# Three transformer blocks on one core: the norms' per-token sums kept as columns, the next norm's sum derived from known sums, and the first unit after a norm from raw fp32 weights

## The chip, the cores and the metric

The kernel runs on one core of a Trainium2 chip, in one launch. Its time is the device time in microseconds, the median of several executions. The engines of the core work in parallel and wait for each other through semaphores: TensorE (PE) multiplies, VectorE (DVE) and ScalarE (ACT) work element by element, GpSimd (POOL) does too, and SyncE (SP) issues the transfers from memory. TensorE's results go to PSUM, which has eight banks of 128x512 fp32 here; everything else lies in SBUF.

## The reference

One sequence of 512 tokens, 1024 channels, all in fp32. A first block (a modulated norm, a mixer of dilated attention and a state-space branch, a modulated norm, a feed-forward block with a short convolution) ends with a norm of its own. Then follow two layers of the second kind:

```
def _rmsnorm_2(x, g):
    y = x32 * lax.rsqrt(jnp.mean(x32 * x32, axis=-1, keepdims=True) + RMS_EPS)
    return (y * g.astype(jnp.float32)).astype(x.dtype)

def second_block(...):
    for l in range(DEPTH_2):
        g = norm_g[l]
        f = _swiglu(_rmsnorm_2(x, g[0]), ffn_w_gate[l, 0], ffn_w_up[l, 0], ffn_w_down[l, 0])
        x = x + 0.5 * _rmsnorm_2(f, g[1])
        m = _mixer(_rmsnorm_2(x, g[2]), w_in[l], conv_w[l], pool_w[l], pool_scale[l], w_out[l])
        x = x + _rmsnorm_2(m, g[3])
        f = _swiglu(_rmsnorm_2(x, g[4]), ffn_w_gate[l, 1], ffn_w_up[l, 1], ffn_w_down[l, 1])
        x = x + 0.5 * _rmsnorm_2(f, g[5])
    return x
```

The norms are per token, over the channels. Between the output of one part and the input of the next stand two of them: the one of `f` (or `m`), which needs all of `f`, and the one of the new `x`, which needs the update by the first. The seven places where this happens are called norms 0 to 6 here: norm 0 is the first block's final norm together with the first norm of layer 0; norms 1, 2, 3 stand behind the first feed-forward block, the mixer and the second feed-forward block of layer 0; norms 4, 5, 6 behind those of layer 1. Norm 6 is the end of the kernel and has no next norm.

## The kernel before

**Layout.** Channels lie on the 128 partitions and the 512 tokens along the free axis, so `x`, `f` and `u` are 8 chunks of 128x512. A sum over channels therefore runs across partitions and chunks.

**Split products.** Every large product is done in a rounded fp32 form (fp32r) with both factors split into a high and a low part: for each chunk of 128 input channels three matmuls of 128x128 by 128x512, `w_hi*u_hi`, `w_hi*u_lo` and `w_lo*u_hi` (L381 to L383). A *unit* is all of these for one 128-channel output, summed in one bank, `unit_bank[0]` or `[1]`. Two units are a *pair*, one for each of two weight slots. A unit over 8 chunks has 24 matmuls. Some small sums are done in plain fp32, where a matmul shows as two instructions.

**Weights.** SyncE loads each unit's weights to `raw[s]`. ScalarE rounds them to `w_hi` (`refill`, L699), once TensorE has finished with the slot. GpSimd subtracts, `w_lo = raw - w_hi` (`split_pair`, L332). The unit on TensorE waits for that and for its bank to have been taken by VectorE (`taken`).

**A feed-forward block of the two layers** runs in two halves of 11 hidden chunks. The hidden units come as pairs (gate, up); VectorE multiplies both by `rstd`, the per-token factor of the norm (L1415, L1417), ScalarE applies the activation and rounds (`h_hi`, L905), and VectorE subtracts for `h_lo` (L1422). The factor is applied to the outputs of the units because the units read x times the gain, without it. Then `down` runs 8 units over the 11 chunks of the half. VectorE takes each bank: `f` is copied in the first half (L1396), added in the second (L1393). **The mixer** has 10 input pairs, attention, convolution and pooling between them, and an output projection of 8 units over 8 chunks, whose banks are copied to `f` (L1396). The first block has a feed-forward block of the same shape with 8 chunks a half.

**A norm** (1 to 5). While the last 8 units run, ScalarE squares each taken chunk (L880) and VectorE adds the square to `acc` (L1400). After the last, TensorE sums `acc` over the partitions with a matrix of ones (`f_sum`, L441), so that each of 128 rows of `stat_bank` has all 512 sums. ScalarE takes the root (L709), VectorE the reciprocal of 128x512 (L1116) and then, for each chunk, the update: `f*g*rstd` to a buffer (L1376) and its addition to `x` (L1377). Behind each updated chunk ScalarE rounds `x*gain` to `u_hi` (L869) and squares `x` (L705), VectorE subtracts for `u_lo` (L1362, `low_part`), and GpSimd adds the squares (`add_squares`, L344 and L347). TensorE runs the first pair chunk by chunk, as the chunks come, into the banks `score`, holding both weight slots until its end (`first_pair`, L420 to L422); behind it the sum of squares of `x` (L427), from which ScalarE and VectorE make the next `rstd`. Norm 0 differs: the products of `down` are written over `x` (L1306), and the squares of `x` are summed by TensorE in fp32 between the units (`unit_and_square`); final norm at L1351. Norms 3 and 0 end in the head of a loop turn over the layers.

**What sets the order.** It is written out by hand: one program per engine, in which a semaphore count stands before each step. SyncE's queue is in the order of use and waits for a `raw` slot. Loops over layers, halves and units are hardware loops.

## Time and profile before

| | |
|---|---|
| runs | 2871.98, 2873.22, 2876.57 us |
| median | 2873.22 us |
| span of the profiled execution | 2864.1 us |
| TensorE busy, matmul | 2611.8 us, 91% |
| TensorE weight loads, beside the matmuls | 2053.4 us, 72% |
| VectorE busy | 1366.7 us, 48% |
| ScalarE busy | 915.4 us, 32% |
| GpSimd busy | 1071.6 us, 37% |

The page gives no time for the profiled execution other than its span, which leaves out what lies around the program. In a timeline every line is one instruction or a row of equal ones: its start in us from the start of the span, its length, the engine, the line in the code, output and inputs, the shape and the count. In brackets stands the idle time of the engine just before, with the operation that ended it. PEclk is the granted clock of TensorE as a share of full speed.

### The profile page before, as it was taken

How to read it: one execution, taken by the hardware profiler on the slowest of the kernel's cores; microseconds unless marked ns; L12 is line 12 of the kernel's file. 1: busy time of each engine (PE TensorE's matmuls, PEld its weight loads, DVE VectorE, ACT ScalarE, POOL GpSimd, SP SyncE). 2: the span in 40 equal slices, each digit the busy share in tenths (PEclk: the TensorE clock that was granted, in tenths of full speed). 3: DMA queues.
4: the chain of work that ended last, by engine and by line, in shares of the span. 5: the costliest groups of instructions: out<-in, count | busy, mean ns of one | idle time of the engine just before them, and what ended most of it. 6: DMA issues, size and time to landing. Idle time of an engine off the chain costs nothing.

```text
span 2864.1 us, 34463 instructions
## 1 busy us (share of the span) xinstructions
PE 2611.8 (91%) x11068; PEld 2053.4 (72%) x11068; DVE 1366.7 (48%) x1956; ACT 915.4 (32%) x1265; POOL 1071.6 (37%) x436
## 2 busy tenths in 40 slices
PE   4988888999799999799799999599997999799997
PEld 2566676888678887576578888488885676588885
DVE  6887667535342232766443132532234656532233
ACT  3333333523332232443332232322233442332231
POOL 1222233444444444322344444344444222444442
PEclk8899899999899999999899999799999999999998
DMA  4111145222123222111122222122231111123231
GB/s 199 52 51 51 42 173 196 95 95 95 59 95 107 84 102 89 45 51 52 66 81 102 89 98 100 46 95 103 89 107 61 52 59 52 66 95 103 88 106 70
DMA packets 63564, 247.74 MB, mean 86 GB/s; under 512 B 7056, under 2 KB 7056, under 8 KB 62224
## 3 DMA queue, kind: packets, MB, share of 16 engines
q1 hardware_dynamic: 63504, 247.01, 24.7%
q8 instruction: 29, 0.48, 0.1%
q14 instruction: 31, 0.25, 0.0%
HBM read 244.89 MB, written 2.10 MB: 86 GB/s over the span
## 4 chain that ended last, share of the span: by engine, by line
PE 66%; issue 21%; DVE 6%; POOL 5%; ACT 1%; DVEq 0%; POOLq 0%; ACTq 0%
PE unit_bank L381 21%; PE unit_bank L383 21%; PE unit_bank L382 21%; POOL w_lo L332 3%; POOL arena L347 2%; PE out_bank L488 1%; DVE rstd L1116 1%; PE score L478 1%; DVE arena L1033 1%; PE score L475 1%; DVE arena L1507 1%; DVE arena L1505 1%; DVE arena L1494 0%; DVE arena L1495 0%; DVE arena L1376 0%
## 5 line engine op out<-in xcount | busy, mean ns | idle before, releaser
L332 POOL TENSOR_TENSOR w_lo<-raw,w_hi 128x1024 fp32r<-128x1024 f32 (+2 forms) x390 | 1006.0, 2581 | 1695.6 <-ACT w_hi L699 1695.6
L381 PE MATMUL unit_bank<-u_hi,w_hi 128*128 128x512 f32 x2160 | 858.5, 397 | 27.5 <-POOL w_lo L332 18.7
L382 PE MATMUL unit_bank<-u_lo,w_hi 128*128 128x512 f32 x2160 | 849.0, 393 | 0.0
L383 PE MATMUL unit_bank<-u_hi,w_lo 128*128 128x512 f32 x2160 | 848.3, 393 | 0.0
L699 ACT ACTIVATE w_hi<-raw 128x1024 fp32r<-128x1024 f32 (+2 forms) x390 | 430.0, 1105 | 1129.9 <-PE unit_bank L383 1083.3
L381 PEld LDWEIGHTS unit_bank<-u_hi,w_hi 128*128 128x128 f32 x2160 | 410.7, 190 | 140.5 <-POOL w_lo L332 27.9
L383 PEld LDWEIGHTS unit_bank<-u_hi,w_lo 128*128 128x128 f32 x2160 | 410.3, 190 | 87.2
L382 PEld LDWEIGHTS unit_bank<-u_lo,w_hi 128*128 128x128 f32 x2160 | 410.7, 190 | 85.6 <-issue 1.4
L381 PE MATMUL unit_bank<-h_hi,w_hi 128*128 128x512 f32 x992 | 390.6, 394 | 5.3 <-DVE h_lo L1566 3.6
L382 PE MATMUL unit_bank<-h_lo,w_hi 128*128 128x512 f32 x992 | 386.7, 390 | 0.0
L383 PE MATMUL unit_bank<-h_hi,w_lo 128*128 128x512 f32 x992 | 386.6, 390 | 0.0
L1417 DVE TENSOR_TENSOR arena<-unit_bank,rstd 128x512 f32<-128x512 f32 x84 | 58.1, 692 | 397.7 <-PE unit_bank L383 397.7
L381 PEld LDWEIGHTS unit_bank<-h_hi,w_hi 128*128 128x128 f32 x992 | 186.5, 188 | 48.4 <-DVE h_lo L1566 4.4
L382 PEld LDWEIGHTS unit_bank<-h_lo,w_hi 128*128 128x128 f32 x992 | 186.7, 188 | 40.0 <-issue 1.7
L383 PEld LDWEIGHTS unit_bank<-h_hi,w_lo 128*128 128x128 f32 x992 | 186.6, 188 | 39.1
L1422 DVE TENSOR_TENSOR h_lo<-arena,h_hi 128x512 f32 (+1 forms) x88 | 169.9, 1931 | 79.2 <-ACT h_hi L905 79.2
L1396 DVE COPY f<-unit_bank 128x512 f32 x48 | 33.2, 692 | 250.0 <-PE unit_bank L383 250.0
L420 PE MATMUL score<-u_hi,w_hi 128*128 128x512 f32 x96 | 46.0, 479 | 100.7 <-DVE u_lo L1362 100.5
L1415 DVE TENSOR_TENSOR arena<-unit_bank,rstd 128x512 f32<-128x512 f32 x84 | 58.1, 691 | 112.3 <-PE unit_bank L383 112.3
L880 ACT ACTIVATE arena<-f 128x512 f32 (+1 forms) x48 | 30.3, 632 | 251.0 <-DVE f L1393 184.3
L420 PEld LDWEIGHTS score<-u_hi,w_hi 128*128 128x128 f32 x96 | 20.7, 215 | 122.7 <-DVE u_lo L1362 119.3
L1393 DVE TENSOR_TENSOR f<-unit_bank,f 128x512 f32 x32 | 22.2, 693 | 152.4 <-PE unit_bank L383 152.4
(238 smaller groups left out, 2370.5 us busy)
## 6 DMA issues: line engine op xcount, KB each, us to landing
raw<-in_w_gate_up SPq DMA_DIRECT2D x176, 512.0 KB, 3.2
raw<-in_w_down SPq DMA_DIRECT2D x64, 704.0 KB, 4.0
raw<-in_w_in SPq DMA_DIRECT2D x70, 512.0 KB, 3.2
f<-in_w_ada_rows SPq DMA_DIRECT2D x32, 512.0 KB, 4.9
raw<-in_w_up SPq DMA_DIRECT2D x32, 512.0 KB, 3.3
raw<-in_w_out SPq DMA_DIRECT2D x24, 512.0 KB, 3.3
ada_w<-in_w_ada SPq DMA_DIRECT2D x8, 1024.0 KB, 7.4
raw<-in_w_down SPq DMA_DIRECT2D x16, 512.0 KB, 3.3
```

Of the source, the lines that this page charges most:

```text
L332: e.tensor_tensor(w_lo[:, s, 0:n], raw[:, s, 0:n], as32(w_hi[:, s, 0:n]), ALU.subtract).then_inc(lo_ready, 1)
L347: e.tensor_tensor(acc, acc, sq[:, c % 2, :], ALU.add).then_inc(sq_used, 1)
L381: e.matmul(bank[:], wh, hi(k), start=n == 0, stop=False)
L382: e.matmul(bank[:], wh, lo(k), start=False, stop=False)
L383: mm = e.matmul(bank[:], wl, hi(k), start=False, stop=last)
L420: e.matmul(into[s][:], wh, u_hi[:, c, :], start=c == 0, stop=False)
L699: e.activation(w_hi[:, s, 0:n], raw[:, s, 0:n], ACT.Copy).then_inc(hi_ready, 1)
L880: e.activation(sq[:, 0, :], f[:, bass.ds(c, 1), :].rearrange("p a t -> p (a t)"), ACT.Square).then_inc(fsq_ready, 1)
L1396: e.tensor_copy(fc, unit_bank[s][:]).then_inc(taken[s], 1)
L1415: e.tensor_tensor(ffn_g, banks[0][:], rstd[:], ALU.mult).then_inc(taken[0], 1)
L1417: e.tensor_tensor(ffn_u, banks[1][:], rstd[:], ALU.mult).then_inc(taken[1], 1)
L1422: e.tensor_tensor(flat(h_lo[:, bass.ds(i, 1), :]), ffn_h, as32(flat(h_hi[:, bass.ds(i, 1), :])), ALU.subtract).then_inc(h_ready, 1)
```

## The change

**Sums as columns.** `sq`'s place in the buffers is divided anew. Each norm's sums are now done with the data as the stationary operand and one column of ones as the moving one (`token_sums`): four products, one for each 128 tokens, give a [128, 4] tile with one token per partition. The root and the reciprocal work on this tile. Where the factor is needed along the free axis, `spread` multiplies the broadcast column by the identity, four products of 128 columns, which gives the 128x512 form in PSUM.

**The next norm's sum from known sums.** With new `x` = `x + g*f*inv`, the sum of squares of the new `x` is the old sum plus 2 times the sum of `x*g*f` times `inv` plus the sum of `(g*f)^2` times `inv` squared. So while the last 8 units run, ScalarE makes a second square, `(g*f)^2` (`gf_sq`), and VectorE adds it to `gf_acc`, makes `x*g*f` (`cross`) and adds that to `cross_acc`; for norm 0 only `gf` is there. `add_squares` and the squares of `x` are gone, and the old sum is kept in `x_sum`. The last chunk's square of `f` is summed by its own products and not added to `f_acc` first.

**The first unit pair in fp32.** The raw weights of the first pair of each part go by transfers of their own (`load_first`) to `first_raw`, a stage ahead, and stay unsplit. `u_all` holds x times the gain in fp32. The pair is 16 plain fp32 products into the `score` banks. The two weight slots pass it by, so the pairs behind it are counted one fewer per part. `u_hi` is rounded from `u_all` by ScalarE, and the eight subtractions for `u_lo` stand behind all eight updates. The first half of the update is written to a `unit_bank` in PSUM instead of a buffer in SBUF, and reads the factor from `stat_bank`.

The loops over the layers are written out, and the activation tables are loaded at set places.

```diff
+        f_sq, gf_sq, f_acc, cross, cross_acc, gf_acc = (slot(n) for n in range(6))
+        f_sum, root_f, root_u, inv_f, inv_u, grown = (slot(11)[:, 128 + 4 * n:132 + 4 * n] for n in range(6))
+        x_sum = stat[:, 0:TB]
+        u_all = slots(16, 8)
+        first_raw = arena[:, 12 * T:16 * T].rearrange("p (s n) -> p s n", s=2)
...
+            def load_first(m, w, first):
+                for s in range(2):
+                    if m:
+                        e.wait_ge(first_done, 2 * (m - 1) + s + 1)
+                    e.dma_start(first_raw[:, s, :], w[first + s]).then_inc(first_loaded[s], 16)
...
+                        e.wait_ge(cat_ready, 4 * l + 4)
+                        load_first(3 * l + 2, d["w_gate_up"], 4 * HALF2 * (2 * l + 1))
+                        load_pairs(mix2(l) + MIX2_IN + 2, d["w_out2"], DC * l + 4, DC // 2 - 2)
...
-                            split_pair(ffn2(l, s), D)
-                            add_squares(3 + 3 * l + 2 * s)
...
+            def token_sums(bank, at, src, apart=1):
+                for b in range(TB):
+                    n = at + apart * b
+                    mm = e.matmul(bank[:, n:n + 1], src[:, b * P:(b + 1) * P], tab("ones", 0, 1), start=True,
+                                  stop=True)
+                return mm
+            def spread(n, inv, bank):
+                e.wait_ge(inverse_ready, n)
+                for b in range(TB):
+                    mm = e.matmul(bank[:, b * P:(b + 1) * P], inv[:, b:b + 1].broadcast_to([P, P]), tab("ident"),
+                                  start=True, stop=True)
+                mm.then_inc(spread_ready, 1)
+            def norm(r):
+                e.wait_ge(fsq_added, (DC - 1) * (r + 1))
+                token_sums(out_bank, 0, f_acc, 2)
+                e.wait_ge(fsq_ready, 2 * DC * r + (2 if r < NORMS - 1 else 1) * (DC - 1) + 1)
+                token_sums(out_bank, 1, f_sq, 2).then_inc(sums_ready, 1)
+                spread(2 * r + 1, inv_f, stat_bank)
+                if r == NORMS - 1:
+                    return
+                e.wait_ge(cross_ready, r + 1)
+                mm = token_sums(mix[0], 0, gf_acc)
+                if r:
+                    mm = token_sums(mix[0], TB, cross_acc)
+                mm.then_inc(cross_sums, 1)
+                for s in range(2):
+                    e.wait_ge(first_loaded[s], 16 * (r + 1))
+                for c in EIGHT:
+                    e.wait_ge(u_full, DC * r + c + 1)
+                    for s in range(2):
+                        mm = e.matmul(score[s][:], first_raw[:, s, c * P:(c + 1) * P], u_all[:, c, :],
+                                      start=c == 0, stop=c == DC - 1)
+                        if c == DC - 1:
+                            mm.then_inc(first_done, 1)
+                    if c == 5:
+                        spread(2 * r + 2, inv_u, mix[1])
...
-                            first_pair(p0, 2 + 3 * l + k_norm, 3 + 3 * l + k_norm, score)
-                            in_unit(p0 + 1, 0, free=0)
-                            in_unit(p0 + 1, 1, free=0)
+                            unit(p0 + 1, 0, from_u, from_u_lo, EIGHT, before=u_chunk(3 * l + k_norm))
+                            in_unit(p0 + 1, 1)
...
-                    f_sum(3 * l + k_norm)
+                    norm(3 * l + k_norm + 1)
...
+            def token_root(out, src):
+                e.activation(out, src, ACT.Sqrt, bias=eps[:], scale=1.0 / D).then_inc(root_ready, 1)
+            def f_squares(p, s, part, c, g):
+                e.wait_ge(taken[s], p + 2)
+                settled()
+                fc = part[:, bass.ds(c, 1), :].rearrange("p a t -> p (a t)")
+                e.activation(f_sq, fc, ACT.Square).then_inc(fsq_ready, 1)
+                if g is not None:
+                    e.activation(gf_sq, fc, ACT.Square, scale=g(c)).then_inc(fsq_ready, 1)
+            def norm(r, p, part, g):
+                ahead = r < NORMS - 1
+                g = g if ahead else None
+                with e.Fori(0, DC // 2 - 1) as i:
+                    for s in range(2):
+                        f_squares(p + i, s, part, 2 * i + s, g)
+                        refill(p + i + 1, s, D if r in (2, 5) or r == 0 else RING)
+                p = p + DC // 2 - 1
+                f_squares(p, 0, part, DC - 2, g)
+                if ahead:
+                    refill(p + 1, 0)
+                f_squares(p, 1, part, DC - 1, g)
+                e.wait_ge(f_summed, r + 1)
+                token_root(root_f, f_sum)
+                if not ahead:
+                    return
+                refill(p + 1, 1)
+                for c in range(DC):
+                    e.wait_ge(x_ready, DC * r + c + 1)
+                    e.activation(u_all[:, c, :], x[:, c, :], ACT.Identity,
+                                 scale=col("norm_g", 2 * r * DC + c)).then_inc(u_full, 1)
+                    e.wait_ge(u_full, DC * r + c + 1)
+                    e.activation(u_hi[:, c, :], u_all[:, c, :], ACT.Copy).then_inc(uhi_ready, 1)
+                    if c == 3:
+                        e.wait_ge(grown_ready, r + 1)
+                        token_root(root_u, grown)
+                e.wait_ge(spread_ready, 2 * r + 2)
+                e.activation(rstd[:], mix[1][:], ACT.Copy).then_inc(rstd_ready, 1)
...
+            def norm(r, p, take, part, g, update):
+                ahead, crossed = r < NORMS - 1, 0 < r < NORMS - 1
+                e.memset(f_acc, 0.0)
+                if ahead:
+                    e.memset(gf_acc, 0.0)
+                if crossed:
+                    e.memset(cross_acc, 0.0)
...
+                def add_gf(c):
+                    e.wait_ge(fsq_ready, 2 * (DC * r + c) + 2)
+                    step(e.tensor_tensor(gf_acc, gf_acc, gf_sq, ALU.add))
+                def chunk(p, s, c, last):
+                    e.wait_ge(unit_done, 2 * p + s + 1)
+                    take(p, s, c)
+                    if crossed:
+                        e.wait_ge(taken[s], p + 2)
+                        settled()
+                        step(e.scalar_tensor_tensor(cross, row(x, c), g(c), row(f, c), ALU.mult, ALU.mult))
+                        step(e.tensor_tensor(cross_acc, cross_acc, cross, ALU.add))
+                    if last:
+                        return
+                    e.wait_ge(fsq_ready, 2 * DC * r + (2 if ahead else 1) * c + 1)
+                    step(e.tensor_tensor(f_acc, f_acc, f_sq, ALU.add))
+                    if ahead:
+                        add_gf(c)
+                    e.sem_inc(fsq_added, 1)
+                with e.Fori(0, DC // 2 - 1) as i:
+                    turn = step.enter(i, 2 * ((2 if crossed else 0) + 1 + ahead))
+                    for s in range(2):
+                        chunk(p + i, s, 2 * i + s, False)
...
+                p = p + DC // 2 - 1
+                chunk(p, 0, DC - 2, False)
+                chunk(p, 1, DC - 1, True)
+                e.wait_ge(sums_ready, r + 1)
+                e.tensor_reduce(f_sum, out_bank[:, 0:2 * TB].rearrange("p (b n) -> p b n", n=2),
+                                mybir.AxisListType.X, ALU.add).then_inc(f_summed, 1)
+                e.wait_ge(root_ready, 2 * r + 1)
+                e.reciprocal(inv_f, root_f).then_inc(inverse_ready, 1)
+                if ahead:
+                    add_gf(DC - 1)
+                    e.sem_inc(cross_ready, 1)
+                e.wait_ge(spread_ready, 2 * r + 1)
+                for c in range(DC):
+                    update(c)
+                    if c == 1 and ahead:
+                        e.wait_ge(cross_sums, r + 1)
+                        gf_sum, cross_sum = mix[0][:, 0:TB], mix[0][:, TB:2 * TB]
+                        step(e.tensor_tensor(grown, gf_sum, inv_f, ALU.mult))
+                        if r:
+                            step(e.scalar_tensor_tensor(grown, cross_sum, 2.0, grown, ALU.mult, ALU.add))
+                            step(e.tensor_tensor(grown, grown, inv_f, ALU.mult))
+                            step(e.tensor_tensor(x_sum, x_sum, grown, ALU.add))
+                        else:
+                            step(e.tensor_tensor(x_sum, grown, inv_f, ALU.mult))
+                        e.tensor_copy(grown, x_sum).then_inc(grown_ready, 1)
+                    if c == 5 and ahead:
+                        e.wait_ge(root_ready, 2 * r + 2)
+                        e.reciprocal(inv_u, root_u).then_inc(inverse_ready, 1)
+                if not ahead:
+                    return
+                for c in range(DC):
+                    e.wait_ge(uhi_ready, DC * (2 + r) + c + 1)
+                    e.tensor_tensor(u_lo[:, c, :], u_all[:, c, :], as32(u_hi[:, c, :]),
+                                    ALU.subtract).then_inc(u_ready, 1)
+                e.wait_ge(rstd_ready, r + 1)
...
+            def post_norm(g):
+                def update(c):
+                    step(e.scalar_tensor_tensor(unit_bank[c % 2][:], f[:, c, :], g(c), stat_bank[:], ALU.mult,
+                                                ALU.mult))
+                    e.tensor_tensor(x[:, c, :], unit_bank[c % 2][:], x[:, c, :], ALU.add).then_inc(x_ready, 1)
+                return update
```

In the instructions of TensorE, the end of the first feed-forward block of layer 0 (norm 1) reads so before; `arena` is the buffer that holds `acc`, and `tabs` the ones:

```order
L383 MATMUL unit_bank<-h_hi,w_lo 128x512
L434 REGISTER_ALU
L434 COMPARE_AND_BRANCH
L440 ISA
L441 MATMUL stat_bank<-arena,tabs 128x512
L413 ISA
L415 REGISTER_ALU
L417 REGISTER_ALU
L420 MATMUL score<-u_hi,w_hi 128x512
L421 MATMUL score<-u_lo,w_hi 128x512
L422 MATMUL score<-u_hi,w_lo 128x512
```

and so after, where `out_bank` receives the sums of `f` and `mix` those for the next norm, then the second factor, and `score<-arena` is the fp32 pair:

```order
L402 MATMUL unit_bank<-h_hi,w_lo 128x512
L498 REGISTER_ALU
L498 COMPARE_AND_BRANCH
L449 MATMUL out_bank<-tabs,arena 128x1 x8
L457 MATMUL stat_bank<-tabs,arena 128x128 x4
L449 MATMUL mix<-tabs,arena 128x1 x8
L483 MATMUL score<-arena 128x512 x12
L457 MATMUL mix<-tabs,arena 128x128 x4
L483 MATMUL score<-arena 128x512 x4
L400 MATMUL unit_bank<-u_hi,w_hi 128x512
L401 MATMUL unit_bank<-u_lo,w_hi 128x512
L402 MATMUL unit_bank<-u_hi,w_lo 128x512
```

The single wide sum is replaced by 8 one-column products and a spread, 8 more one-column products stand before the first pair, the pair has 16 products and a second spread inside it, and the first ordinary unit follows it directly, with no sum between.

VectorE, one chunk of the mixer's output projection (norm 2) before:

```order
L1396 ISA
L1396 COPY f<-unit_bank 128x512
L1398 ISA
L1399 ISA
L1400 TENSOR_TENSOR arena<-arena 128x512
L1391 REGISTER_ALU
```

and after, where the second row is the take, `x,cols,f` makes `cross`, and the adds are those of `cross_acc`, `f_acc` and `gf_acc`:

```order
L1504 ISA
L1504 COPY f<-unit_bank 128x512
L1438 REGISTER_ALU
L1440 ISA
L1440 SCALAR_TENSOR_TENSOR arena<-x,cols,f 128x512
L91 ISA
L1441 TENSOR_TENSOR arena<-arena 128x512
L91 REGISTER_ALU
L1444 ISA
L1445 TENSOR_TENSOR arena<-arena 128x512
L91 REGISTER_ALU
L1431 ISA
L1432 TENSOR_TENSOR arena<-arena 128x512
```

Between one take and the next VectorE has four further steps where it had one.

VectorE between the last take of norm 1 and its first updates, before:

```order
L1388 REGISTER_ALU
L1388 COMPARE_AND_BRANCH
L1115 REGISTER_ALU
L1116 RECIPROCAL rstd<-arena 128x512
L90 REGISTER_ALU
L1376 ISA
L1376 SCALAR_TENSOR_TENSOR arena<-f,half_g,rstd 128x512
L90 REGISTER_ALU
L1377 TENSOR_TENSOR x<-x,arena 128x512
```

and after:

```order
L1500 TENSOR_TENSOR f<-unit_bank,f 128x512
L1440 SCALAR_TENSOR_TENSOR arena<-x,half_g,f 128x512
L1441 TENSOR_TENSOR arena<-arena 128x512
L1459 TENSOR_REDUCE arena<-out_bank 128x4
L1462 RECIPROCAL arena<-arena 128x4
L1432 TENSOR_TENSOR arena<-arena 128x512
L1517 SCALAR_TENSOR_TENSOR unit_bank<-f,half_g,stat_bank 128x512
L1519 TENSOR_TENSOR x<-unit_bank,x 128x512
```

The wide reciprocal gives way to a reduction and a reciprocal of 128x4; two cross steps stand ahead of them, the last add of `gf_acc` behind them, and the update's first half goes to PSUM.

## Rows read from the trace of the kernel before

**Rows 1.** Busy time by stretches: length, then PE, PEld, DVE, ACT, POOL, PEclk, DMA, GB/s

```profile
core 0 of [0], span 2864.1 us
800.00:1138.00 338.00, 338.00 (x1493) 279.88 (x1492) 100.40 (x106) 91.92 (x104) 149.90 (x56) 1.00 0.28 97
...
1138.00:1193.00 55.00, 35.57 (x129) 23.55 (x128) 42.57 (x61) 23.93 (x40) 20.36 (x11) 0.88 0.13 47
```

**Rows 2.** Timeline of TensorE at norm 1: start, us, operation, [idle before <- what ended it]

```profile
1138.55 0.39 PE L383 MATMUL unit_bank<-h_hi,w_lo 128*128 128x512 f32 x1
1141.32 2.07 PE L441 MATMUL stat_bank<-arena,tabs 128*128 128x512 f32 x2 [2.38 <-DVE arena L1400]
1151.25 0.79 PE L420 MATMUL score<-u_hi,w_hi 128*128 128x512 f32 x1 [7.85 <-DVE u_lo L1362]
...
1154.86 0.39 PE L421 MATMUL score<-u_lo,w_hi 128*128 128x512 f32 x1
...
1175.66 0.50 PE L381 MATMUL unit_bank<-u_hi,w_hi 128*128 128x512 f32 x1 [2.12 <-POOL w_lo L332]
```

**Rows 3.** Timeline of VectorE and ScalarE at the same norm, columns as before

```profile
1139.10 0.69 DVE L1393 TENSOR_TENSOR f<-unit_bank,f 128x512 f32 x1 [5.24 <-PE unit_bank L383]
...
1139.83 0.63 ACT L880 ACTIVATE arena<-f 128x512 f32<-128x512 f32 x1 [5.89 <-DVE f L1393]
...
1144.15 3.35 DVE L1116 RECIPROCAL rstd<-arena 128x512 f32<-128x512 f32 x1 [2.88 <-ACT arena L709]
1147.67 0.75 DVE L1376 SCALAR_TENSOR_TENSOR arena<-f,half_g,rstd 128x512 f32<-128x512 f32 x1 [0.16 <-DVE rstd L1116]
1148.45 0.69 DVE L1377 TENSOR_TENSOR x<-x,arena 128x512 f32<-128x512 f32 x1
...
1149.32 0.72 ACT L869 ACTIVATE u_hi<-x,cols 128x512 fp32r<-128x512 f32 x1 [4.25 <-DVE x L1377]
```

**Rows 4.** Timeline of VectorE and TensorE at norms 0, 3 and 5

```profile
756.68 0.75 DVE L1306 SCALAR_TENSOR_TENSOR x<-unit_bank,mod,x 128x512 f32 x1 [5.60 <-PE unit_bank L383]
...
790.43 0.50 PE L381 MATMUL unit_bank<-u_hi,w_hi 128*128 128x512 f32 x1 [2.12 <-POOL w_lo L332]
...
1794.55 0.69 DVE L1393 TENSOR_TENSOR f<-unit_bank,f 128x512 f32 x1 [5.24 <-PE unit_bank L383]
...
1842.41 0.50 PE L381 MATMUL unit_bank<-u_hi,w_hi 128*128 128x512 f32 x1 [2.12 <-POOL w_lo L332]
...
2457.74 0.69 DVE L1396 COPY f<-unit_bank 128x512 f32 x1 [3.19 <-PE unit_bank L383]
...
2493.37 0.50 PE L381 MATMUL unit_bank<-u_hi,w_hi 128*128 128x512 f32 x1 [2.12 <-POOL w_lo L332]
```

**Rows 5.** Timeline: short fp32 sums on TensorE and one small VectorE add

```profile
41.72 6.99 PE L531 MATMUL out_bank<-tabs,ada_acc 128*128 128x1 f32 x32 [14.81 <-DVE ada_acc L1097]
48.74 0.17 DVE L1103 TENSOR_TENSOR mod<-out_bank,cols 128x16 f32<-128x16 f32 x1 [7.08 <-PE out_bank L531]
...
491.23 1.84 PE L539 MATMUL out_bank<-tabs,ada_sums 128*128 128x1 f32 x16
...
787.29 1.02 PE L427 MATMUL stat_bank<-arena,tabs 128*128 128x512 f32 x2
...
1358.61 1.88 PE L512 MATMUL score<-arena,pool_w 128*128 128x512 f32 x4
```

**Rows 6.** Timeline of ScalarE and GpSimd in the mixer's output projection

```profile
1381.51 0.63 ACT L880 ACTIVATE arena<-f 128x512 f32 x1 [3.85 <-DVE f L1396]
1382.05 1.04 ACT L699 ACTIVATE w_hi<-raw 128x1024 fp32r<-128x1024 f32 x1
...
1383.17 2.40 POOL L332 TENSOR_TENSOR w_lo<-raw,w_hi 128x1024 fp32r<-128x1024 f32 x1 [3.04 <-ACT w_hi L699]
```

**Rows 7.** Timeline of GpSimd and VectorE in a hidden stage

```profile
1458.28 2.54 POOL L332 TENSOR_TENSOR w_lo<-raw,w_hi 128x1024 fp32r<-128x1024 f32 x1 [2.97 <-ACT w_hi L699]
...
1459.48 1.88 DVE L1422 TENSOR_TENSOR h_lo<-arena,h_hi 128x512 f32 x1 [0.92 <-ACT h_hi L905]
```

302 lines of the change are left out of this document (129 added, 173 removed).

## The prediction

> **What bounds the kernel now.** I read the span and the busy time by stretches first, then the timeline of one norm. In the hidden and down products of a feed-forward block TensorE is busy for the whole stretch, 338.0 of 338 us. The 55 us at a norm hold 35.6 us of busy TensorE at a granted clock of 0.88 [rows 1]. So time can be won only at the seven norms, and any delay put into the stretches between them is paid in full.
>
> The timeline of the norm at 1139 us shows what a norm costs. The last product of the down projection starts at 1138.55 and takes 0.39 us, so I count from E = 1138.94. TensorE then runs one sum, starts the first pair at 1151.25 and the first ordinary unit at 1175.66 [rows 2], which is 36.7 us after E. Only 48 products of 0.227 us, 10.9 us, lie in it. The rest is a chain [rows 3]: take of the last bank (0.16 us after E), square, add, the fp32 sum on TensorE, square root, a reciprocal over 128x512 of 3.35 us, the first update at E + 8.7, and the first rounded chunk at E + 10.4. Then the first pair goes at VectorE's pace, and after it the two weight slots that it held are split again: the last idle before 1175.66 is 2.12 us for `w_lo` [rows 2].
>
> The other norms read the same way. The take starts 0.16 us after E, so E follows from it. Of the four norms of this pattern (r = 1, 2, 4, 5) the first needs 36.7 us and the last, 2457.58 to 2493.37, 35.8 us; the mean of the four is 36.2. Norm 3, between the layers, needs 1794.39 to 1842.41, 48.0 us. Norm 0 needs 756.52 to 790.43, 33.9 us [rows 4].
>
> **The change, part by part.** I build the new stretch from E to the first ordinary unit.
>
> 1. Start of the chain. The take and the square are as before: the square ends at E + 1.52 [rows 3]. The sums of the seven earlier chunks run meanwhile. The last square is summed by four one-column products, 8 instructions: 0.115 us each warm, 0.22 us each cold [rows 5], 0.9 or 1.8 us. The clock is at half in the old sum at 1141.32, since its two instructions take 2.07 us against 1.02 warm [rows 2, 5], so it falls about there: I take the middle, E + 2.9.
> 2. The reduction, the root and the reciprocal work on 128x4 in place of 128x512. No such row exists; the nearest is an add of 128x16 from PSUM, 0.17 us [rows 5]. With hand-overs of 0.05 us the three take 0.75 us: E + 3.65. The 3.35 us reciprocal is gone.
> 3. The spread of the inverse is 8 instructions of 128 columns, bounded by 0.115 each (one column, warm) and a quarter of a cold 512-column one (1.03 / 4 = 0.26). I take 0.25, cold: E + 5.65. Norm 6 ends with its updates from here; they stood at E + 8.7, so the tail shortens by 3.0 us.
> 4. Before the first pair TensorE also sums `gf_acc` and `cross_acc`, 16 one-column instructions, 3.5 us cold: E + 9.2. In norm 0 only 8 of them stand there: E + 7.4. The first update and add (0.75 + 0.69) and ScalarE's 0.72 give the first chunk of u by E + 8 [rows 3], so the sums decide.
> 5. The first pair is now 16 fp32 products, 32 instructions. Two take 1.02 us and four 1.88 [rows 5], so one more costs 0.43, and 32 of them 13.8 us in place of 10.9. The clock: before, the first pair starts cold at 1151.25 and is warm (0.39 us) at 1154.86, at most 3.6 us later [rows 2]. Where the rise falls hangs on chance, so I take somewhat more, 4.2 us (bounds 3 and 6); at half speed 2.1 us of them are lost. The second spread adds 0.95. Sum 16.8 us: E + 26.0, in norm 0 E + 24.2.
> 6. VectorE is not later. An update and its add are 1.44 us, the step between them 0.03 [rows 3]; eight from E + 5.65, with 1.5 us of small steps, end at E + 19. The eight subtractions for `u_lo` (0.69 each) then run ahead of TensorE, which needs the first at E + 26. GpSimd no longer adds up the squares of x, and so doesn't collide with VectorE there. The weights of the next pair are split early, since the first pair no longer holds their slots; the 2.12 us wait goes. If VectorE had to write the updates to PSUM at more than 2.2 us each, it would be the bound (a rival).
>
> Gains: four norms at 36.2 - 26.0 = 10.2, 40.8 us; norm 3 at 48.0 - 26.0 = 22.0; norm 0 at 33.9 - 24.2 = 9.7; the tail 3.0. In the down products of norm 0, TensorE also loses the interleaved fp32 sums: chunks come every 5.60 + 0.75 = 6.35 us (the wait for the bank and its take) [rows 4], against 24 x 0.2264 = 5.43 for 24 products by [rows 1], where 1493 take 338 us. Five such periods are 4.6 us. Together 80.1 us.
>
> 7. What the down products pay. Each chunk now has a second square on ScalarE ahead of the weights' rounding, and up to three more VectorE steps. In the output projection of the mixer, 8 k-tiles, a unit is 5.43 us. Rounding starts 0.54 us after the square and `w_lo` 1.12 us after that, for 2.40 us [rows 6]. With the square at 0.73 after the take the split ends 4.8 us after it; a second square makes that 5.4, and the weights are needed 5.3 after it. Norm 0 has the same: about 0.2 us for six units, 1.2 us. The 11 k-tiles of the feed-forward blocks (7.47 us a unit) have room.
> 8. In the mixer's output VectorE itself is the larger cost. After the take come cross (0.75), its add, the f add and the gf add, each 0.69 with about 0.15 between in the loop: the gf add would start 3.4 us after the take, just after `w_lo` starts (3.2). An `h_lo` subtraction of two SBUF inputs that starts inside a `w_lo` of 1458.28 to 1460.82 takes 1.88 us instead of 0.69 and ends 0.54 us after it [rows 7]. So I let the gf add end 0.5 us after a split that ends at 5.7: the next take comes 6.2 us after this one, where 5.43 were due. Over seven chunks this is 5.1 us, in each of two mixers. In the feed-forward blocks the same add ends at 7.4 us, within the 7.47. Losses: 10.2 + 1.2 = 11.4 us.
>
> The row shows the add held until the split ends. The Trainium skill, page "SBUF — State Buffer", section "Who interferes with whom", says the same as a rule: the shared port pair belongs to whichever of the two starts first, for its whole instruction. By it point 8 costs 5.1 us a mixer; if both engines simply ran side by side it would cost only the 1.2 us of point 7, and the sum would be 7.8 us lower. It also speaks against this change in one more place, the last gf add at a norm: should the split of slot 1 start before it, all that follows moves by 1.9 us.
>
> Other edits cost nothing: the first weights are two loads more to a queue with DMA engines idle for most of the time, issued a stage ahead (in the mixer after `cat_ready`, eight units or 43 us before use); the table loads are moved under the down products; the loop over layers is written out, one more fetch of instructions; memsets (0.48 each) fall into VectorE's wait before the first chunk.
>
> **The sum.** 2864.1 - 80.1 + 11.4 = 2795.4 us of span. The page gives no time for the profiled execution beyond its span; the median of the runs, 2873.22, is 9.1 above it. I predict 2804.5 us.
>
> **The rivals.**
> - *The clock stays up.* If the small sums are enough to keep it, or it returns earlier, points 1, 3, 4 and 5 lose 0.3, 1.1, 1.7 and 2.1 us: 5.2 a norm, 31 us over six, 2773. Against it: one-column products ran for 7 us at 0.22 us each without becoming faster [rows 5].
> - *VectorE becomes the bound.* Updates that write to PSUM have no row. At 0.69 + 0.75 they are hidden; at 2.4 us an update pair, or with the last gf add locked out, a norm costs 2 to 4 us more: 2817 to 2829.
> - *The fp32 pair stays cold* (slower than before). If the clock didn't return during it, its 32 instructions cost 27.6 us in place of 15.9, the second spread 1 us more, and the next unit starts cold, 2 us more: 14.6 a norm, 88 us over six, 2892. It decides from a first pair of over 27 us. Against: the earlier first pair warmed within 3.6 us, though VectorE made it wait in between.
> - *The change is hidden by the weights.* If something else released the first ordinary unit (its weights, or the `u_lo` of the last chunks) the norms would stay near 36 us, and only the tail and norm 0 would win: 2873.2 - 7.6 + 11.4 = 2877. Nothing in the rows points there.
>
> **How the numbers follow.** Chances: the forecast (2790 to 2817) 0.62, the clock up 0.15, VectorE bound 0.15, cold 0.05, hidden 0.03. The range from 2776 to 2832 takes in the first three nearly whole. About 0.2% is what a measurement of this kernel can tell from no change: faster by more 0.92, within it 0.03, slower 0.05.
>
> **What would show it.** From the last product of a down projection to the first ordinary unit 26 us (24 in norm 0); the first fp32 product at about E + 9, the last warm; chunks of the mixer's output every 6.2 us; the gf add of those chunks at about 2.8 us instead of 0.69; the first update at E + 5.7. Wrong: a first pair that waits for `u_all` (VectorE bound), a wait for `w_lo` in the feed-forward down products, or a start of the chain at full clock.

## The result: 2799.22 us, 2.6% less, and the profile after

The changed kernel takes 2799.22 us (median of 4 runs, 2793.74 to 2800.65) where the kernel before took 2874.89 in the same series: ratio 0.9739, 95% interval 0.9718 to 0.9759. The forecast was 2804.5, with a range of 2776 to 2832. The profiled execution has a span of 2796.1 us, 68.0 less than before; the sum in the prediction gave 2795.4.

The busy time of two stretches of the changed kernel, the columns as in [rows 1], which they answer:

```profile
core 0 of [0], span 2796.1 us
790.00:1128.00 338.00, 338.00 (x1490) 279.11 (x1489) 115.56 (x128) 98.27 (x114) 152.44 (x56) 1.00 0.30 99
1132.00:1187.00 55.00, 53.47 (x212) 36.42 (x211) 42.10 (x97) 28.15 (x54) 7.11 (x3) 0.94 0.12 39
```

Between the norms of the feed-forward blocks nothing has changed: TensorE is busy throughout, at full clock (a granted clock of 1.00, that is 2.4 GHz; *warm* below means this, *cold* means half of it). The 55 us from norm 1 on hold 53.5 us of TensorE instead of 35.6. TensorE at that norm, which answers [rows 2]:

```profile
1133.12 0.95 PE L449 MATMUL out_bank<-tabs,arena 128*128 128x1 f32 x8
1134.73 1.05 PE L449 MATMUL out_bank<-tabs,arena 128*128 128x1 f32 x8 [0.66 <-ACT arena L768]
1136.65 1.47 PE L457 MATMUL stat_bank<-tabs,arena 128*128 128x128 f32 x8 [0.87 <-DVE arena L1462]
1137.91 3.41 PE L449 MATMUL mix<-tabs,arena 128*128 128x1 f32 x16
1141.18 12.03 PE L483 MATMUL score<-arena 128*128 128x512 f32 x24
1153.05 1.05 PE L457 MATMUL mix<-tabs,arena 128*128 128x128 f32 x8
1153.93 3.60 PE L483 MATMUL score<-arena 128*128 128x512 f32 x8
1156.97 0.79 PE L400 MATMUL unit_bank<-u_hi,w_hi 128*128 128x512 f32 x1
```

and VectorE there, which answers [rows 3]:

```profile
1133.32 0.69 DVE L1500 TENSOR_TENSOR f<-unit_bank,f 128x512 f32<-128x512 f32 x1 [3.82 <-PE unit_bank L402]
...
1135.89 0.17 DVE L1459 TENSOR_REDUCE arena<-out_bank 128x4 f32<-128x8 f32 x1 [0.36 <-PE out_bank L449]
1136.42 0.18 DVE L1462 RECIPROCAL arena<-arena 128x4 f32<-128x4 f32 x1 [0.36 <-ACT arena L761]
...
1138.15 0.76 DVE L1517 SCALAR_TENSOR_TENSOR unit_bank<-f,half_g,stat_bank 128x512 f32<-128x512 f32 x1 [0.98 <-PE stat_bank L457]
...
1150.61 4.90 DVE L1489 TENSOR_TENSOR u_lo<-arena,u_hi 128x512 fp32r<-128x512 f32 x8
```

With E = 1133.16 (0.16 us ahead of the take, as before) the first update starts at E + 5.0, the fp32 pair at E + 8.0 and the first ordinary unit at E + 23.8, waiting for nothing but the pair. VectorE's eight subtractions end before the pair does. The longest idle time of TensorE left in it is 0.87 us.

In this trace the last product of the down projection itself ends at 1133.28, 0.04 us and not 0.16 ahead of the take. The lengths of the norms in the table and from here on are counted from that end; for the changed kernel and its variants they are therefore 0.12 us shorter than counted from the take (23.7 for 23.8 here), while for the kernel before both ways agree.

Where the 68.0 us come from, in the two profiled executions, beside the terms of the prediction (minus is a gain):

| stretch | predicted | measured |
|---|---|---|
| norm 0, E to first unit (34.0 to 23.1) | -9.7 | -10.9 |
| norms 1, 2, 4, 5 (144.6 to 97.9) | -40.8 | -46.8 |
| norm 3 (48.0 to 25.4) | -22.0 | -22.6 |
| norm 6, E to the end (22.3 to 18.1) | -3.0 | -4.1 |
| down products of norm 0 | -3.4 | -1.9 |
| the two mixers, first ordinary unit to E | +10.2 | +10.3 |
| the four feed-forward blocks, the same | 0 | +1.9 |
| the first 720 us, code that is unchanged | 0 | +6.2 |
| sum | -68.7 | -67.9 |

So the close hit is in part misses that cancel, which is luck: the norms gave 8.9 us more than I counted (some 0.7 of it by the way of counting the end), 6.2 us went in code that the change does not touch, and 3.4 us in down products that were counted too cheap.

### The profile page after: what moved, and what is told of

Its sections match the earlier page's. It is cut to its first block, busy times and chain, and to the rows that moved or that the text cites. A ratio compares the mean times of both kernels' runs of the same rounds, so it can differ in the third digit from the quotient of the medians.

```text
span 2796.1 us, 33914 instructions
## 1 busy us (share of the span) xinstructions
PE 2655.5 (95%) x11236; PEld 2076.7 (74%) x11236; DVE 1406.6 (50%) x2132; ACT 934.4 (33%) x1307; POOL 988.6 (35%) x382
## 4 chain that ended last, share of the span: by engine, by line
issue 70%; POOL 15%; PE 14%; POOLq 1%; DVE 0%; ACT 0%; DVEq 0%
POOL w_lo L365 15%; PE unit_bank L400 4%; PE unit_bank L401 4%; PE unit_bank L402 4%; PE score L483 1%; POOLq L369 1%; DVE x L1519 0%; DVE unit_bank L1517 0%; POOLq L364 0%; PE stat_bank L457 0%; PE mix L449 0%; PE out_bank L449 0%; ACT arena L768 0%; PE mix L457 0%; DVE f L1504 0%
## 5 line engine op out<-in xcount | busy, mean ns | idle before, releaser
L365 POOL TENSOR_TENSOR w_lo<-raw,w_hi 128x1024 fp32r<-128x1024 f32 (+2 forms) x378 | 988.4, 2615 | 1780.4 <-ACT w_hi L751 1780.4
L751 ACT ACTIVATE w_hi<-raw 128x1024 fp32r<-128x1024 f32 (+2 forms) x378 | 418.0, 1106 | 1086.1 <-PE unit_bank L402 1071.1
L400 PE MATMUL unit_bank<-h_hi,w_hi 128*128 128x512 f32 x992 | 390.8, 394 | 16.2 <-POOL w_lo L365 10.9
L1504 DVE COPY f<-unit_bank 128x512 f32 (+1 forms) x48 | 33.2, 692 | 213.4 <-PE unit_bank L402 206.9
L483 PE MATMUL score<-arena 128*128 128x512 f32 x192 | 98.2, 671 | 0.4 <-ACT arena L793 0.4
L1500 DVE TENSOR_TENSOR f<-unit_bank,f 128x512 f32 (+1 forms) x32 | 22.1, 692 | 117.2 <-PE unit_bank L402 117.2
L483 PEld LDWEIGHTS score<-arena 128*128 128x128 f32 x192 | 41.0, 220 | 48.8 <-issue 47.1
```

The costliest lines, as they stand in the source:

```text
L365: e.tensor_tensor(w_lo[:, s, 0:n], raw[:, s, 0:n], as32(w_hi[:, s, 0:n]), ALU.subtract).then_inc(lo_ready, 1)
L400: e.matmul(bank[:], wh, hi(k), start=n == 0, stop=False)
L483: mm = e.matmul(score[s][:], first_raw[:, s, c * P:(c + 1) * P], u_all[:, c, :], start=c == 0, stop=c == DC - 1)
L751: e.activation(w_hi[:, s, 0:n], raw[:, s, 0:n], ACT.Copy).then_inc(hi_ready, 1)
L1504: e.tensor_copy(flat(f[:, bass.ds(c, 1), :]), unit_bank[s][:]).then_inc(taken[s], 1)
```

## Experiments

Each variant has 4 to 12 timed executions, with the kernel before timed beside it. Four sets were timed together: the first four variants; `all_psum`, `filler`, `b_noadds` and `late_split`; `b_filler`, `b_cols` and `all_psum_filler`; and `filler_gaps`. Within a set medians are compared, across sets the ratios to the kernel before. How a variant's time divides over stretches is read from its one profiled execution.

**The changed kernel once more.** No edit.

> The changed kernel once more, beside its variants. Two theories on the 6.2 us by which its first 520 us (code that the change doesn't touch) were longer than in the profile of the kernel before: (chance) the half-speed stretches of the granted clock fall differently from one execution to the next there; then this profile puts the start of the last product before the first norm anywhere between 757 and 764 us, and the median is 2799 again; (layout) the changed program causes it; then it is within 1 us of 760.6 again and the profile of every variant with it. Norms: 23 to 26 us from the last down product to the first ordinary unit, as in the first profile.

Measured: 2795.56 us, ratio 0.9728 (0.9714 to 0.9742), span 2792.3. E of norm 0 stands at 754.2 us, against 760.6 in the first profile, and so even earlier than the 757 to 764 of the theory of chance. In the ten profiles of the changed kernel and its variants this point lies between 754.2 and 762.2 us, with no pattern in the edits (the two largest, 762.2 and 762.1, belong to variants that do better in the down products of norm 0), and in the four of the kernel before and its variants between 756.4 and 763.0. So the 6.2 us do not belong to the changed program: the same program moved by 6.4 us, and its half-speed stretches ahead of this point add up to 136.5 us in the first profile and to 122.9 in the second. The norms of this profile are 23.0, 25.4, 25.4, 25.4, 23.7 and 25.2 us: each of norms 1 to 5 is either about 23.7 or about 25.3, and norm 1 has changed sides since the first profile. Variants that differ by a few us are therefore compared by stretches as well.

**Where the mixers lose 10 us: the sum of g\*f squared in PSUM.**

```diff
-                    e.memset(gf_acc, 0.0)
+                    e.memset(mix[1][:], 0.0)
...
-                    step(e.tensor_tensor(gf_acc, gf_acc, gf_sq, ALU.add))
+                    step(e.tensor_tensor(gf_acc if isinstance(c, int) and c == DC - 1 else mix[1][:], mix[1][:], gf_sq,
+                                         ALU.add))
```

> The running sum of the squares of g*f is kept in a PSUM bank (mix[1]) and only its last add writes SBUF; the work is the same. Theory 1 (the add waits for GpSimd's w_lo because both have SBUF inputs): in the mixer's output the add takes 0.7 us instead of 2.72, and chunks come every 5.7 us instead of 6.47 and 6.72 in turn, the rest being the late w_lo; 6 us less in each of two mixers, 12 us in all. Theory 2 (the weights are late because the second square stands ahead of their rounding, and the add's wait is hidden beside that): the chunks stay at 6.5 us, and the time within 2 us of the changed kernel's. Norm 0 and the feed-forward blocks the same by both.

Measured: 2782.41 us, 13.2 less than the changed kernel beside it, ratio 0.9682 (0.9668 to 0.9697). VectorE in the output projection of norm 2 in the changed kernel:

```profile
1352.90 2.72 DVE L1432 TENSOR_TENSOR arena<-arena 128x512 f32<-128x512 f32 x1 [0.16 <-DVE arena L1445]
1356.04 0.69 DVE L1504 COPY f<-unit_bank 128x512 f32 x1 [0.42 <-DVE arena L1432]
...
1362.77 0.69 DVE L1504 COPY f<-unit_bank 128x512 f32 x1 [0.70 <-DVE arena L1432]
```

and GpSimd there:

```profile
1352.68 2.38 POOL L365 TENSOR_TENSOR w_lo<-raw,w_hi 128x1024 fp32r<-128x1024 f32 x1 [10.40 <-ACT w_hi L751]
```

The add starts 0.22 us after `w_lo`, takes 2.72 us and ends 0.56 us behind its end, and the take that follows was waiting for VectorE, not for TensorE. With the sum in PSUM, VectorE:

```profile
1353.01 0.69 DVE L1505 COPY f<-unit_bank 128x512 f32 x1 [1.45 <-PE unit_bank L402]
...
1356.32 0.70 DVE L1432 TENSOR_TENSOR mix<-mix,arena 128x512 f32<-128x512 f32 x1
1359.12 0.69 DVE L1505 COPY f<-unit_bank 128x512 f32 x1 [2.10 <-PE unit_bank L402]
...
1364.56 0.69 DVE L1505 COPY f<-unit_bank 128x512 f32 x1 [1.43 <-PE unit_bank L402]
```

and GpSimd:

```profile
1356.11 2.38 POOL L365 TENSOR_TENSOR w_lo<-raw,w_hi 128x1024 fp32r<-128x1024 f32 x1 [3.08 <-ACT w_hi L751]
```

The same add, again 0.2 us into a `w_lo`, takes 0.70 us. Theory 1 holds; the first six intervals between takes are 5.8 us on average instead of 6.6. The gain at the mixers is smaller than the 12 us that were expected, though: from the first ordinary unit to E the two take 232.7 and 232.6 us, for 236.7 and 236.8 in the first profile of the changed kernel and 237.6 and 236.8 in the second, so 8 to 9 us together. The four feed-forward blocks, for which nothing was expected, are 2.4 us shorter together: in three of them every second unit of the down projection had started some 0.2 us late, and no longer does. The remaining 3 to 5 us of this profile lie at the norms, four of whose five are of the short kind; whether the edit has a part in that or chance alone, no run separates. The Trainium skill, page "SBUF — State Buffer", section "Who interferes with whom", has this limit of its rule too: outside its two-port modes, a VectorE instruction with at most one SBUF input does not contend with GpSimd. The trace agrees, 0.70 against 2.72 us.

**Only the order on ScalarE.**

```diff
                 e.activation(f_sq, fc, ACT.Square).then_inc(fsq_ready, 1)
+                if between:
+                    between()
                 if g is not None:
...
-                        f_squares(p + i, s, part, 2 * i + s, g)
-                        refill(p + i + 1, s, D if r in (2, 5) or r == 0 else RING)
+                        f_squares(p + i, s, part, 2 * i + s, g,
+                                  lambda: refill(p + i + 1, s, D if r in (2, 5) or r == 0 else RING))
```

> Only the order on ScalarE: the rounding of the next weights stands between the two squares of a chunk instead of behind both. Theory 1 (the add's wait sets the chunk time): w_lo starts 0.6 us earlier and ends 4.9 us after the take, the add is held until 5.4 and the next take comes at 5.8, so 0.8 us less a chunk, 11 us over both mixers, and 3 us in norm 0, where the chunks alternate between 6.3 and 5.45 us: 14 us. Theory 2 (late weights set it): chunks of 5.45 us everywhere, 19 us less.

Measured: 2791.25 us, 4.3 less than the changed kernel beside it, ratio 0.9706 (0.9691 to 0.9721), an interval that overlaps the one of the changed kernel. Both expectations were too high. GpSimd there:

```profile
1352.33 2.94 POOL L365 TENSOR_TENSOR w_lo<-raw,w_hi 128x1024 fp32r<-128x1024 f32 x1 [9.79 <-ACT w_hi L751]
```

and VectorE:

```profile
1352.32 0.69 DVE L1447 TENSOR_TENSOR arena<-arena 128x512 f32<-128x512 f32 x1
1353.17 2.65 DVE L1434 TENSOR_TENSOR arena<-arena 128x512 f32<-128x512 f32 x1 [0.16 <-DVE arena L1447]
1356.24 0.69 DVE L1506 COPY f<-unit_bank 128x512 f32 x1 [0.42 <-DVE arena L1434]
```

The split starts 2.5 us after the take, as hoped, but at the moment at which VectorE's add of the squares of f begins, and then takes 2.94 us instead of 2.38: the lock works in the other direction too. `w_lo` starts 0.6 us earlier after the take and takes 0.56 longer, so that it ends 5.43 us after it instead of 5.49, and takes come every 6.40 and 6.65 us instead of 6.47 and 6.73. The mixers are only 1 to 2 us shorter together (236.3 each); the rest of this profile's gain lies in the feed-forward blocks (2.3 us) and at the norms, and is not shown to come from the chunks of the mixer. In norm 0 the chunks even became slower, 5.87 us on average for 5.78.

**Both together.** The two diffs above.

> The sum in PSUM and the rounding between the squares together. By theory 1 neither is left: chunks every 5.45 us in the mixers (7.7 us less in each) and in norm 0 (3 us less): 18 us less than the changed kernel, and 4 to 6 us less than either edit alone. By theory 2 the same as the new order alone.

Measured: 2782.55 us, ratio 0.9675 (0.9661 to 0.969): the same as the sum in PSUM alone, not 4 to 6 us less. The `w_lo` of 2.9 us is still there.

**All three running sums in PSUM.** In addition to both:

```diff
-                e.memset(f_acc, 0.0)
+                e.memset(stat_bank[:], 0.0)
...
-                    e.memset(cross_acc, 0.0)
+                    e.memset(mix[0][:], 0.0)
...
-                        step(e.tensor_tensor(cross_acc, cross_acc, cross, ALU.add))
+                        step(e.tensor_tensor(cross_acc if last else mix[0][:], mix[0][:], cross, ALU.add))
...
-                    step(e.tensor_tensor(f_acc, f_acc, f_sq, ALU.add))
+                    step(e.tensor_tensor(f_acc if isinstance(c, int) and c == DC - 2 else stat_bank[:], stat_bank[:],
+                                         f_sq, ALU.add))
```

> All three running sums (f, cross, g*f squared) in PSUM banks, their last adds alone into SBUF, and the rounding between the squares. With gf's sum alone in PSUM the split still started when VectorE's add of the squares of f stood in its way (2.92 us instead of 2.38). If two SBUF inputs are what locks, in both directions: w_lo takes 2.4 us from 2.5 after the take, TensorE never waits for weights, chunks come every 5.45 us in the mixers and in norm 0 instead of 5.5 and 6.04 in turn: 2.4 us less for each of three places, 7 us less than `both`, near 2775. If the 6.04 comes from the loop's own overhead (branch and fetch in each turn of two units) it stays, and the time is that of `both`, 2782.

Measured: 2782.77 us, ratio 0.969 (0.9675 to 0.9704): no gain in time over the one sum in PSUM. In its trace the mechanism did what was expected: no wait for weights is left in the mixer's output, `w_lo` takes 2.40 us, and the chunks come 5.44 to 5.53 us apart where `both` had 5.5 and 6.04 in turn, so the 6.04 us were the lock and not the loop. From the first ordinary unit to E a mixer takes 231.8 us instead of 236.8, as before the change (232.3 and 230.9). But `both` has 233.4 and 233.3 there, and of the 3 us that this gives 2.6 were lost in this profile at the norms, four of whose six were of the long kind (24.9 to 25.4). Why the medians of five executions agree as well is not shown. The next experiment turns to what makes a norm long or short.

**The clock at the norms.** Products that nothing reads, in TensorE's waits:

```diff
+            def filler(n):
+
+                for _ in range(n):
+                    e.matmul(score[0][:], h_hi[:, 0, 0:P], h_hi[:, 1, :], start=True, stop=True)
...
                 token_sums(out_bank, 0, f_acc, 2)
+                filler(3)
...
                 token_sums(out_bank, 1, f_sq, 2).then_inc(sums_ready, 1)
+                filler(4)
...
                 mm.then_inc(cross_sums, 1)
+                filler(4)
```

> Eleven fp32r products of 128x512 whose result nothing reads stand in the waits of TensorE at each norm: 3 behind the first sums (0.68 us in a gap of 0.66), 4 behind the last square's sums (0.9 us in 0.87), 4 behind the sums for the next norm, before the fp32 pair. Theory A (the clock falls because TensorE is almost idle from the last down product to the fp32 pair, and useful or useless products there keep it): the granted clock stays at full speed through norms 0 to 5, the pair starts 7.2 us after E instead of 7.9 and takes 14.7 us with its spread instead of 16 to 17.6; first unit 22 us after E instead of 23 to 25.4: 12 to 18 us less than the changed kernel. Theory B (the clock falls anyway, by what happened before E or by chance): the fillers run cold, push the pair back by up to 1.7 us, and the time is 5 to 12 us more.

Measured: 2779.39 us, ratio 0.9677 (0.9663 to 0.969) against the 0.9728 of the changed kernel, some 15 us less. Stretches of the changed kernel and of this one that hold norm 1, and norm 3, in the columns of [rows 1]:

```profile
1134.00:1158.00 24.00, 22.47 (x76) 13.74 (x76) 19.63 (x40) 15.19 (x23) 2.36 (x1) 0.86 0.09 31
1769.00:1794.00 25.00, 23.47 (x76) 14.11 (x75) 19.52 (x37) 15.19 (x23) 2.36 (x1) 0.80 0.09 33
```

```profile
1129.00:1150.00 21.00, 21.00 (x85) 12.39 (x85) 19.09 (x38) 15.20 (x23) 2.36 (x1) 1.00 0.11 38
1759.00:1780.00 21.00, 21.00 (x84) 12.29 (x84) 19.16 (x36) 15.15 (x23) 2.36 (x1) 1.00 0.10 34
```

The granted clock stays at 1.00, that is 2.4 GHz, where the changed kernel has a mean of 0.86 and 0.80. TensorE at norm 1:

```profile
1134.37 1.18 PE L464 MATMUL score<-h_hi 128*128 128x512 f32 x4
1135.38 10.54 PE L491 MATMUL score<-arena 128*128 128x512 f32 x24
1145.76 1.05 PE L457 MATMUL mix<-tabs,arena 128*128 128x128 f32 x8
1146.65 3.60 PE L491 MATMUL score<-arena 128*128 128x512 f32 x8
```

The first 24 instructions of the pair take 10.54 us instead of 12.03 at norm 1 and 13.41 at norm 3. Norm 0 takes 20.5 us and the five others 21.4 to 21.5, all alike. The change made the norms dense, the longest wait is under 1 us (0.87 at norm 1, 0.95 at norm 2), and still the clock fell there: the one-column instructions (16 before the spread, 16 behind it) and the spread's own 8 do not hold it, and eleven wide products among them do. Whether the waits or the narrow products let it fall is not separated, since the fillers stand in both.

**Which of them are needed.** The last four left out.

> Like `filler`, without its last 4 products, which stood behind the 16 one-column products for the next norm's sum; the 3 and the 4 ahead of them stay. Theory A1 (the clock is lost in the waits between E and the first spread, 1.5 us of idle and 16 small products): these 7 keep it, and the norms stay at 20.5 and 21.4 us: 2780 us. Theory A2 (the 16 one-column products and the wait for the first chunk of u, 3 us without a large product, are enough to lose it): the granted clock falls in some norms after the spread, these take 23 to 25 us, and the time lies between 2785 and 2796.

Measured: 2786.45 us, ratio 0.9696 (0.9683 to 0.9709). That is some 5 us more than with all eleven by the ratios, whose intervals just overlap. In its profile norms 0, 1 and 3 take 20.5, 21.4 and 21.4 us, and norms 2, 4 and 5 take 22.9, 22.9 and 22.7. The stretch of norm 4:

```profile
2127.00:2151.00 24.00, 23.26 (x93) 14.21 (x93) 19.92 (x38) 15.16 (x23) 2.85 (x2) 0.93 0.14 44
```

Neither pure case: the first seven are enough at half of the norms, and where they are not, about half of the loss stays away (1.4 us over 21.4 where the changed kernel has 2.3 or 3.9). So both places can lose the clock. That chance decides which one does in a given norm is a guess from one profile.

**Would the clock have paid before the change?** The same products in the kernel before, 10 ahead of the wide sum and 34 behind it:

```diff
             def f_sum(r):
 
+                filler(10)
                 e.wait_ge(fsq_added, (DC + 1) * (r + 1))
                 e.matmul(stat_bank[:], tab("ones"), acc, start=True, stop=True).then_inc(fsum_ready, 1)
+                filler(34)
```

> The kernel before with filler products in the two waits of TensorE at norms 1 to 6: 10 ahead of the wide sum (2.3 us in a gap of 2.4) and 34 behind it (7.7 us in one of 7.9). The clock then stays up to the first pair. Theory (there the pair goes at VectorE's pace, so the clock matters little): only the wide sum is quicker, 2.07 to 1.02 us, and the first chunk: 1 to 1.5 us a norm, 6 to 9 us less than the kernel before. Rival (the clock costs as much before as after the change): 2 to 3 us a norm, 15 us less.

Measured: 2871.63 us beside 2870.71, ratio 0.9999 (0.9989 to 1.0009): nothing, and less than the 6 to 9 us of the theory. TensorE at norm 1:

```profile
1143.19 1.13 PE L447 MATMUL stat_bank<-arena,tabs 128*128 128x512 f32 x2
1143.75 8.31 PE L441 MATMUL score<-h_hi 128*128 128x512 f32 x34
1155.24 0.50 PE L420 MATMUL score<-u_hi,w_hi 128*128 128x512 f32 x1 [1.40 <-DVE u_lo L1369]
```

The wide sum is quick (1.13 us for 2.07), and the pair waits 1.4 us for every second chunk. Norms 1, 2, 4 and 5 take 35.7 to 35.8 us where they took 35.8 to 36.7. With VectorE setting the pace, TensorE's clock is worth under 1 us a norm; with TensorE setting it, 3. The zero has a second part. The stretch that begins with the first ordinary unit behind norm 1, in the columns of [rows 1]:

```profile
1176.50:1190.00 13.50, 13.46 (x49) 10.04 (x50) 9.54 (x21) 5.76 (x14) 4.70 (x2) 0.87 0.33 106
```

The clock stood at 1.00 until there and then fell for 3.4 us, under products that TensorE does back to back, at 0.43 us instead of 0.23 for each. In this profile it does so behind norms 1, 2, 4 and 5, in the kernel before behind norm 2 only, and the mixer behind norm 1 takes 1.4 us longer for it. With the waits of the pair left in place, the fillers in part moved the fall of the clock from a place where it costs nothing to one where it does.

**What held the pair before: GpSimd's adds.**

```diff
-                        e.tensor_tensor(acc, sq[:, 0, :], sq[:, 1, :], ALU.add).then_inc(sq_used, 2)
+                        e.tensor_tensor(acc[:, 0:1], sq[:, 0, 0:1], sq[:, 1, 0:1], ALU.add).then_inc(sq_used, 2)
...
-                        e.tensor_tensor(acc, acc, sq[:, c % 2, :], ALU.add).then_inc(sq_used, 1)
+                        e.tensor_tensor(acc[:, 0:1], acc[:, 0:1], sq[:, c % 2, 0:1], ALU.add).then_inc(sq_used, 1)
```

> The kernel before, with GpSimd's seven adds of the squares of x at each norm cut to one column of 512, so that the sum behind the next rstd is wrong; all waits and instructions stay. It prices what these adds cost VectorE, whose steps take 1.66 to 1.77 us instead of 0.7 seven times a norm. Theory (TensorE's first pair goes at VectorE's pace, and the lock by GpSimd sets that): the first pair ends 6 us earlier at norms 1 to 5 (norm 0 has no updates between), 30 us less than the kernel before, 2843 to 2846. Rival (ScalarE's square and rounding in turn set the pace, or the pair is held by its own length): less than 10 us less.

GpSimd's seven adds now take one column of 512, so this kernel leaves out most of the sum of squares of `x` behind the next `rstd`, and its output is not the reference's.

Measured: 2836.1 us, 37 less than the kernel before, ratio 0.9874 (0.9859 to 0.989). This is 7 to 10 us below what was expected; its profile has 31.5 us of it at the norms, and the rest is not located. Norm 1 takes 29.7 us instead of 36.7 (0.95 of it ahead of the adds, where the sum of f found the clock still up, 1.13 us for 2.07), norms 1 to 5 together 29.1 less (5.8 each) and norm 0, whose first pair also runs beside these adds, 2.4. At norm 1 of the kernel before six of VectorE's steps take 1.66 to 1.77 us; here the longest, apart from the reciprocal, is 0.75. The adds are gone in the changed kernel too, and about half of the 76 us that the change gives has the size of this part.

**The columns alone,** in the kernel before, for f's sum at norms 1 to 6:

```diff
-                e.matmul(stat_bank[:], tab("ones"), acc, start=True, stop=True).then_inc(fsum_ready, 1)
+                for b in range(TB):
+                    mm = e.matmul(out_bank[:, b:b + 1], acc[:, b * P:(b + 1) * P], tab("ones", 0, 1), start=True,
+                                  stop=True)
+                mm.then_inc(fsum_ready, 1)
+                e.wait_ge(inverse_ready, r + 1)
+                for b in range(TB):
+                    mm = e.matmul(stat_bank[:, b * P:(b + 1) * P], inv_f[:, b:b + 1].broadcast_to([P, P]),
+                                  tab("ident"), start=True, stop=True)
+                mm.then_inc(spread_ready, 1)
...
-                    invert(4 + 6 * l + 2 * k)
+                    e.wait_ge(std_ready, 5 + 6 * l + 2 * k)
+                    e.reciprocal(inv_f, root_f).then_inc(inverse_ready, 1)
+                    e.wait_ge(spread_ready, 3 * l + k + 1)
```

> The kernel before with one part of the change alone: at norms 1 to 6 the sum of f's squares as four one-column products, root and reciprocal on 128x4, spread by four products. The last square is still added on VectorE first. Theory: the chain to the first update goes from 8.7 us after E to about 6.1 (take and square 1.5, add 0.75, sums 0.9 to 1.8, small steps 0.75, spread 1.2 to 1.8, hand-overs), and all behind it moves along: 2.6 us at six norms, 16 us less than the kernel before, 2857. Rival (the first pair's weights, split behind the root at E + 6.2 to 8.5, or the lock against them hold the pair back anyway): less than 5 us.

Measured: 2850.87 us, 20 less than the kernel before beside it where 16 were expected, ratio 0.9925 (0.9909 to 0.9941). Norms 1, 2, 4 and 5 take 33.0 us on average instead of 36.2, norm 3 41.9 instead of 48.0. VectorE at norm 1, whose E is 1145.67:

```profile
1150.26 0.18 DVE L1383 RECIPROCAL arena<-arena 128x4 f32<-128x4 f32 x1 [2.26 <-ACT arena L895]
1152.73 0.75 DVE L1388 SCALAR_TENSOR_TENSOR arena<-f,half_g,stat_bank 128x512 f32<-128x512 f32 x1 [2.29 <-PE stat_bank L449]
```

The first update stands at E + 7.1, 1.7 us earlier and not 2.6, since the spread and its hand-over, on a cold TensorE, take 2.3 us. The rest of what norm 1 gains (36.7 to 33.2 us) is something that I had not counted. Six of VectorE's steps are still held by GpSimd's adds, but two of them had been updates `f*g*rstd` of 1.77 us; these read their factor from PSUM now and take 0.73, and the additions to `x` that are held in their stead take 1.00 us each. The six together lose 4.3 us instead of 6.1.

**The slots that pass the pair by.** In the changed kernel, the roundings moved behind the fp32 pair:

```diff
-                if ahead:
-                    refill(p + 1, 0)
...
-                refill(p + 1, 1)
...
+                e.wait_ge(first_done, 2 * r + 2)
+                for s in range(2):
+                    refill(p + 1, s)
                 e.activation(rstd[:], mix[1][:], ACT.Copy).then_inc(rstd_ready, 1)
```

> One part of the change undone: the two weight slots behind the first pair are rounded and split only when the fp32 pair is done, as before where the pair held them. Theory (the slots that pass the pair by give back the split): the first ordinary unit waits for rounding 1.05, w_lo 2.35 and hand-overs, 3.6 us more at each of six norms, 21 us more than the changed kernel: 2817 to 2821. Rival (the split at the head of the norm costs VectorE's steps as much by the shared lock): less than 10 us more.

Measured: 2826.74 us, ratio 0.9846 (0.9825 to 0.9867), 34 us more than the changed kernel by the ratios. TensorE and GpSimd at norm 1:

```profile
1162.38 0.59 PE L400 MATMUL unit_bank<-u_hi,w_hi 128*128 128x512 f32 x1 [3.62 <-POOL w_lo L365]
```

```profile
1159.97 4.67 POOL L365 TENSOR_TENSOR w_lo<-raw,w_hi 128x1024 fp32r<-128x1024 f32 x2 [34.61 <-ACT w_hi L751]
```

The wait is the 3.6 us that I expected, but the total is 13 us above the expected 21: the six norms lose 25.4 us together and the stages behind them 7.0. TensorE falls to half speed once more behind the idle stretch (3.4 us at each of the six), and `rstd`, which the edit puts behind the roundings, comes later; how the 7.0 us divide between the two was not tested.

**The version with all of it**: three sums in PSUM, the order on ScalarE, eleven fillers.

> The three running sums in PSUM, the rounding between the squares, and the eleven filler products. The two effects lie in different stretches (the down projections, the norms), so they should add up: the norms as in `filler`, 20.5 and five of 21.4 us, the mixers as in `all_psum`, 5 us shorter each: 2779.4 - 13 = 2766 us. Rival (fillers leave too little for what gf's last add and the sums for the next norm wait for): no more than 5 us below `filler`.

Measured: 2762.91 us (2758.20 to 2767.68), ratio 0.9617 (0.9604 to 0.963): 3.8% less than the kernel before and some 32 us less than the changed one by the ratios. VectorE in the output projection of norm 2:

```profile
1351.46 0.69 DVE L1516 COPY f<-unit_bank 128x512 f32 x1 [1.44 <-PE unit_bank L402]
...
1354.79 0.70 DVE L1442 TENSOR_TENSOR mix<-mix,arena 128x512 f32<-128x512 f32 x1
1356.97 0.69 DVE L1516 COPY f<-unit_bank 128x512 f32 x1 [1.48 <-PE unit_bank L402]
```

Takes come 5.45 to 5.57 us apart, the norms take 20.5 and five times 21.4 us. The effects add up, as expected of different stretches: 11 us for `all_psum` and 15 for `filler` by the ratios make 26, and the 32 that came are no further from that than the intervals allow, which reach about 4 us each way for every ratio.

## Why the prediction was right, and which of its terms were off

**The frame held.** The time is won at the norms alone; TensorE is the bound in the new stretch; VectorE is hidden behind the pair; the mixers pay. Each shows in the trace after.

**Points 1 to 3, the chain,** were priced too cold. The clock falls later than in the middle I chose, between E + 3.2 and E + 4.4 at norms 1 to 5: the last square's sums take 1.05 us, warm, at every norm; the spread's eight instructions 1.47 us at norm 1 and not 2.0, but 2.08 at norms 2 and 5. The first update stands at E + 5.0 instead of 5.65 at norm 1 and between E + 4.8 and E + 5.7 over the five, and the tail is shorter by 4.1 us instead of 3.0. The small steps (0.17, 0.30 and 0.18 us with their hand-overs) were right to 0.1.

**Point 4** was right in itself (3.41 us for 3.5), and starts 0.9 us earlier. **Point 5**: the pair with its spread takes 15.8 us at norm 1 and 17.2 at norm 3, for 16.8. The time lost to the clock was right on average; that it comes in two sizes I did not see. **Point 6** holds: updates that write to PSUM take 0.76 and 0.69 us. Sum for a norm: 24.6 us on average over norms 1 to 5, for 26.0. The last gf add, which I feared might be locked out by the split of slot 1, ends 0.22 to 0.24 us ahead of it at each of norms 0 to 5 and takes 0.66 us.

**The gain at a norm as a whole** was the time before, read from rows, less the new time, built up step by step. How it divides among the reciprocal, GpSimd's adds and the early split I had not worked out; the experiments show it: the columns 3.2 us a norm, the adds 5.8, the slots 4.2. They overlap, and the dearer pair (fp32, 2.9 us by the prediction's sum) goes against them.

**Points 7 and 8** named the right mechanism, the add held by `w_lo`, and `gf_psum` shows it: 2.72 us become 0.70, and the mixers get 8 to 9 us back, by one operand's place. The sizes were off, and that 10.3 us came for 10.2 is luck. Seven times 6.2 less 5.43 is 5.4 and not 5.1 us. A chunk, once the add is held, is 6.6 us and not 6.2: of the hand-over from the held add to the next take, 0.42 us and 0.70 in every second turn, I had counted nothing. Against this the first two of the seven intervals of TensorE's units are still 5.5 and 6.2 us, and the kernel before, which I had put at 5.43 throughout, was at 5.5. So the seven take 44.3 and 44.5 us in the two mixers instead of 38.9 and 38.5, which is 11.4 more, and the rest of the first mixer is 1.0 shorter, whose half-speed stretches add up to 6.8 us instead of 10.2. The feed-forward blocks did not quite have room: 1.9 us. In norm 0 the chunks come 5.46 and 6.29 us apart in turn: in every second unit TensorE waits 0.62 us for `w_lo`. Seven periods last 40.5 us where 38.0 were due, so the loss that was put at 1.2 us is 2.5.

**The rivals.** That the clock stays up did not happen; made to happen, it is worth 18.9 us over six norms (146.4 to 127.5) and some 15 in the time, not the 31 I had put on it. About 8 of the 12 us between are that the norms were already that much shorter than forecast; the others are that a norm at full clock takes 21.4 us and not 20.8, because the pair then waits for the first chunk of u: in `filler_gaps`, without products ahead of it, it starts at E + 7.07 and not at E + 6.1. VectorE never bound. The pair did not stay cold: the half-speed stretches last 6.8 or 10.2 us. Hidden by the weights: in `late_split`, where the weights do release the first unit, 34 us go, and this was the only part undone in the changed kernel.

**The base.** The median of the kernel before stood 9.1 us above its profiled execution, and I carried that over. For the changed kernel it is 3.1. The difference fits the chance of the first 720 us: the profile of before was a short one there (756.4), the one of after a long one (760.6, with 1.9 us less work). The second profile and its median differ by 3.3.

## What to carry to other kernels

Before you price a chain of small steps ask who sets the pace of the work behind it: filler products were worth nothing while VectorE paced the first pair, and 15 us once TensorE did. When VectorE and GpSimd work side by side, look at each VectorE step with two SBUF inputs; here a running sum kept in PSUM, with only its last add into SBUF, took it out of GpSimd's way without an instruction more. And after a change that makes a stretch dense, look at the granted clock there: here short waits and narrow products let it fall to half, and eleven wide products in the gaps kept it up. And before you explain a difference of 3 us between two variants, compare them stretch by stretch and profile the same kernel twice.

## What the runs showed of the hardware that was not expected

- The lock works in both directions: a `w_lo` that starts together with a VectorE add of two SBUF inputs takes 2.94 us instead of 2.38.
- A few us of one-column and 128-column products with waits of 0.66 to 0.96 us among them were enough for TensorE's granted clock to fall at each of the six norms in both profiles of the changed kernel; with eleven products of 512 columns in the same place it fell at none of the six, in two kernels.
- Where it falls, it costs one of two sizes: half-speed stretches of 6.8 or 10.2 us, and at norms 1 to 5 lengths of about 23.7 or about 25.2 us. Two profiles of the changed kernel differ in it at norm 1, so a single profile of such a kernel is uncertain by several us for this alone.
